# Two raw weight buffers and five split slots in place of three and four

## The chip, the cores and the metric
The kernel runs on 1 core of one Trainium2 chip, as one program. The metric is the device time of one execution in microseconds; the number given for the kernel before is the median of 3 runs.

## The reference, cut to what matters
Two blocks of a language model act one after the other on one sequence of 256 positions, with a model width of 1024, everything in fp32. What matters here is how many different weight matrices it multiplies with: each is used once, by 256 rows.
```python
def first_block(x, mem, ...):               # x, mem: (1, 256, 1024)
    mem_n = rms_norm(mem, mem_norm_gain)
    for layer in range(2):
        g = norm_gains[layer]
        hn = rms_norm(x, g[0])
        y = mlstm_mixer(hn, ...) if layer == 0 else stick_breaking_mixer(hn, ...)
        x = x + rms_norm(y, g[1])
        y = memory_cross_attention(rms_norm(x, g[2]), mem_n, xa_w_q[layer], xa_w_kv[layer], xa_w_o[layer])
        x = x + rms_norm(y, g[3])
        y = swiglu_ffn(rms_norm(x, g[4]), ffn_w_gate_up[layer], ffn_w_down[layer])   # D_FF 2816
        x = x + rms_norm(y, g[5])
    return x

def second_block(x, mem, ...):
    z = _rmsnorm(x, norm_mix_g) @ w_in
    hq, hf, hi, hg, fq, fk, fv, ff, mq, gate_logits = split(z)
    y_a = _hgrn2_mixer(hq, hf, hi, hg, ...)     # chunkwise gated linear attention
    y_b = _fox_mixer(fq, fk, fv, ff, ...)       # softmax attention with forget gates
    y_c = _memory_mixer(mq, _rmsnorm(mem, ...) @ mem_kv_w, ...)
    merged = sum over the three of sigmoid(gate) * (y @ w_br)
    x = x + merged @ w_out
    return x + _conv_glu_ffn(_rmsnorm(x, norm_ffn_g), ffn_w_up, ..., ffn_w_down)
```

## The kernel before, in words
**Weights as a stream.** All weights come from device memory in fp32, in the fixed order in which they are used. `chunk()` (L174 to L202) is called once for each of 207 chunks. A chunk is 1024 KB, that is [128, 2048] on chip, but for two narrow ones of 8 columns each: `mlg` (gate columns of the mLSTM) and `ff` (forget gates of the fox attention). A wide chunk is cut into two pieces of [128, 1024], a narrow one is one piece; there are 412 pieces. Chunk n lies in raw buffer n % NRAW (`raw` is [128, NRAW, 2048] fp32, L100), piece p in slot p % NSP of `whi` and of `wlo` (each [128, NSP, 1024], L101 and L102). A raw buffer and a slot of the two split tiles take the same 8 KB of a partition.

**The split.** TensorE multiplies in a rounded fp32 form, so each weight w is written as a hi part (w rounded) and a lo part (w minus hi), and each product is three matmuls: hi by hi, hi by lo and lo by hi. ACT makes the hi of each piece (a copy, L1149 in `hi_to`), DVE the lo (a subtraction of hi from raw, L1691 in `lo_to`); PE then uses the piece, in order.

**Who waits for what.** SP's program (L2469 to L2489) issues the loads in order. Before the load of chunk c it waits until DVE has made the last lo of chunk c-NRAW (L2474), then issues it (L2480). The two loads of the memory tokens stand in the same queue, right behind `mlg` (L2483). ACT waits at the first piece of a chunk for the landed data (L1146), and for piece p until PE has used piece p-NSP (L1148). DVE waits for the hi. PE waits for the lo. `w_used` counts the pieces that PE is done with.

**Places written out by hand.** ACT and DVE also do everything else: they clear the banks, and compute norms, activations and softmaxes. Each engine takes its instructions strictly in the order in which the program has them, and where the copies and the subtractions stand in it is written out by hand: `past(name)` stands for "make the pieces up to the last one of chunk `name`, plus NSP more" (L1152 for ACT, L1694 for DVE). A call puts all pieces that are not yet made there, each with its waits. So ACT, at a copy whose data has not landed, stands still with everything behind it.

**The order of the work.** mLSTM: `mlq0`, `mlq1`, `mlg`, `mlk0`, `mlk1`, `mlv0a` to `mlo1b` (queries, gates, keys, values, output gates), the decays with exponentials at L1310 to L1314 on ACT and the column tile `acol` on DVE, and PE's log-decay products at L668. Then cross attention (`xq0_0` and on), a feed-forward (`g0_j`, `u0_j`, `d0_j`: gate, up and down chunk of step j), stick-breaking attention (`sbq`, `sbk`, `sbv`, its softmax on ACT, the output weights `sbo0` and on, transposed values in `sb_values`, PE L789), cross attention again (`xq1_0` and on; squares and `norm_hi` at L1181 on ACT before it), a second feed-forward, the second block's mixers (`hq` to `mq`, the six gate blocks `gate0a` to `gate5b`, the branches, `mo`), and the last feed-forward (`g2_j`, `u2_j`, `d2_j`). At the fox attention ACT copies the turned keys (L1515), and `fox_pair` on PE begins with L988. At the last feed-forward's entry the norm of the second 128 rows is copied on ACT in `tile_hi` (L1661), eight copies, and PE's `first_hi` (L437) does the hi products of the first half before they are there. In a feed-forward, DVE clears the gate banks (L1794) and the up banks (L1807), and ACT copies the product for the down matmuls (L1271).

**The narrow pieces.** A narrow piece writes only 16 of the 128 columns of each k-block of its hi slot, but PE's `gate_rows` (L477 to L485) multiplies with all 128 (`both`), so that the other columns only have to be finite numbers. `mlg` is piece 4: slot 0 before the change, which piece 0 has filled.

**Lines of PE.** L407 to L409 are the matmuls of the query and key blocks, L422 and L424 those of the gate and up chunks, L472 to L474 those of the blocks with rows on the partitions.
Of the kernel before, what the change touches and what calls it, by code (L numbers as in the profile page):

```python
# [8 lines left out]
F32 = mybir.dt.float32  # L9
# [8 lines left out]
FF = 2816  # L18
FT = FF // 128
NJ = FT // 2  # L20
NRAW = 3
NSP = 4
NAMES = """
K_act K_dve V_act V_dve act_step constants dve_step f_act f_cols f_conv f_first f_gate f_hi f_lo f_prod
f_tap2 f_up fb_in fx_e fx_m fx_p fx_pa fx_pd fx_s fx_t fx_v g1_in g2_in g3_in gains gains_T gate gb_in h_A
h_A01m h_cp h_d h_e h_f h_m1 h_m2 h_n h_o h_q h_r h_sq h_z half_sq heads_T heads_a heads_d heads_n hg_act
hn_r hn_sq hn_ss ho_r ho_sq ho_ss lg_zero lo_first m2_act m2_dve mT_T mT_hi mT_lo m_T m_hi m_lo m_r m_sq m_x
mem0_in0 mem0_in1 mem1_in0 mem1_in1 mg mg0 ml_act ml_cols ml_dec ml_dve ml_hs ml_log ml_num ml_og ml_p ml_qk
# [63 lines left out]
def build_program(nc, I, out):  # L92
    ctx = ExitStack()
    with ctx:
        def sb(name, shape, dt=F32):
            return ctx.enter_context(nc.sbuf_tensor(name, shape, dt))


        ps = ctx.enter_context(nc.psum_tensor("ps", [128, 8, 512], F32))
        raw = sb("raw", [128, NRAW, 2048])  # L100
        whi = sb("whi", [128, NSP, 1024], F32R)  # L101
        wlo = sb("wlo", [128, NSP, 1024], F32R)  # L102
        xr = sb("xr", [128, NT, D])
# [70 lines left out]
        def chunk(name, src, cut):  # L174
            n = len(order)
            cols, kt = src.shape[1], src.shape[0] // 128
            view = raw[:, n % NRAW, 0:kt * cols].rearrange("p (k c) -> p k c", c=cols)
            if kt * cols <= 1024:
# [6 lines left out]
            if cols == 8:  # L185
                p = len(pieces)
                both = whi[:, p % NSP, :].rearrange("p (k c) -> p k c", c=128)
                if cut == "g":
# [7 lines left out]
            for v in views:  # L196
                p, k, c = len(pieces), v.shape[1], v.shape[2]
                mine.append(Piece(p, n, v, whi[:, p % NSP, 0:k * c].rearrange("p (k c) -> p k c", c=c),
                                  wlo[:, p % NSP, 0:k * c].rearrange("p (k c) -> p k c", c=c)))
                pieces.append(mine[-1])  # L200
# [89 lines left out]
        S = {}  # L290
# [844 lines left out]
        def scalar_program(act):  # L1135
# [3 lines left out]
            def hi_to(n):  # L1139

                while made[0] < min(n, len(pieces)):
                    p = pieces[made[0]]
                    if p.n == 0:
                        act.wait_ge(S["w_first"], 16)
                    elif p.n == 1 or pieces[p.n - 1].of != p.of:
                        act.wait_ge(S[f"w_raw{p.of % NRAW}"], 16 * (p.of // NRAW + 1))  # L1146
                    if p.n >= NSP:
                        act.wait_ge(S["w_used"], p.n - NSP + 1)  # L1148
                    act.activation(p.hi, p.raw, ACT.Copy).then_inc(S["w_hi"], 1)  # L1149
                    made[0] += 1  # L1150

            def past(name):  # L1152

                hi_to(end(name) + NSP)
# [127 lines left out]
            step(act.activation(junk, mhalf[:, :], ACT.Square))  # L1282
            squares(0)
            hi_to(2)
            act.wait_ge(S["gains"], 1)
            norm_hi(0, gain1(0, 0))
            hi_to(4)


# [1027 lines left out]
        def gpsimd_program(pool):  # L2317
            own = [0]

            def step(i):  # L2320
                own[0] += 1
                i.then_inc(S["pool_step"], 1)
                return own[0]
# [27 lines left out]
                    rstd(hn_st[n][t], nh, 512 // nh, "hn_ss", 2 * n + t + 1, "hn_r")  # L2351


            pool.memset(ident[:, :], 0.0)
            z = step(pool.memset(identb[:, :], 0.0))
            pool.memset(mhalf[:, :], -0.5).then_inc(S["mhalf"], 1)
# [112 lines left out]
        def sync_program(sp):  # L2469
            for t in range(NT):  # L2470
                sp.dma_start(xr[:, t, :], x2[:, t, :]).then_inc(S[f"x_in{t}"], 16)
            for c in order:
                if c.n >= NRAW:
                    sp.wait_ge(S["w_lo"], order[c.n - NRAW].end)  # L2474
                src, sem = c.src.rearrange("(k p) c -> p k c", p=128), S[f"w_raw{c.n % NRAW}"]
                if c.n == 0:
# [28 lines left out]
        @block.gpsimd  # L2505
        def _(e):
            gpsimd_program(e)
# [29 lines left out]
```

## Time and profile before
| | |
|---|---|
| median of 3 runs | 1301.5 us (1301.43 to 1301.62) |
| the profiled execution | 1301.93 us, span in the trace 1299.9 us |
| busy share of the span | PE 99%, weight loads of PE 85%, DVE 68%, ACT 53%, POOL 9% |
| granted TensorE clock | the top digit in all 40 slices, mean 1.0 |
| DMA | 223.62 MB, mean 172 GB/s; the queue of the weight loads keeps 16 DMA engines busy for 51.0% |
| weight loads | 1024 KB each, median 5.1 us from issue to landing (6.5 for those of the mLSTM's `w_in`) |

How to read it: the time of an execution is about 2 us more than the span of its trace. PE has work in all but some 18 us of the span. The slices of the page show where PE has less: the first one of 40, with 7 tenths, and no other. The weight load of a matmul (PEld) runs beside the matmul before it, so its idle time costs nothing as long as PE is busy.

### The profile page before, as it was taken

The numbers are of one execution on the slowest core, as the hardware profiler recorded it, in microseconds if no ns is written. First come the engines' busy times: TensorE is split into PE (matmuls) and PEld (weight loads), VectorE is DVE, ScalarE is ACT, GpSimd is POOL, SyncE is SP. The second block draws the span as 40 slices with busy tenths as digits, with TensorE's granted clock in tenths as the row PEclk, the third lists the DMA queues.
The fourth block names the chain that finished last, engine by engine and source line by source line (L and its number), as shares of the span: only waits on it lengthen the run. The fifth ranks groups of instructions, "written<-read, shape, count | busy, mean of one in ns | idle before, by whom it ended". The sixth has DMA issues, their size and how long they took to land.

```text
span 1299.9 us, 17608 instructions
## 1 busy us (share of the span) xinstructions
PE 1281.9 (99%) x7273; PEld 1106.5 (85%) x7273; DVE 883.7 (68%) x1038; ACT 688.1 (53%) x961; POOL 110.7 (9%) x176
## 2 busy tenths in 40 slices
PE   7999999999999999999999999999999999999999
PEld 7888897988888888888888888898877888888887
DVE  4656664776666776875676666768785566887775
ACT  5755544544444656564554444565566654654453
POOL 6200100100000100030100000101330003000000
PEclk9999999999999999999999999999999999999999
DMA  8754643565555553353365555563544435365552
GB/s 265 258 162 157 204 146 126 178 194 195 193 186 185 181 163 129 131 192 132 130 195 193 189 186 183 182 193 106 162 147 147 160 130 194 131 204 186 193 195 97
DMA packets 156112, 223.62 MB, mean 172 GB/s; under 512 B 6103, under 2 KB 107635, under 8 KB 156032
## 3 DMA queue, kind: packets, MB, share of 16 engines
q1 hardware_dynamic: 154240, 218.18, 51.0%
q0 software_dynamic: 1664, 4.27, 1.0%
q8 instruction: 57, 0.93, 0.3%
q14 instruction: 23, 0.19, 0.1%
q10 hardware_dynamic: 128, 0.05, 0.0%
HBM read 221.44 MB, written 1.05 MB: 171 GB/s over the span
## 4 chain that ended last, share of the span: by engine, by line
PE 85%; DVE 7%; ACT 4%; issue 2%; POOL 1%; DMA 1%; SPq 0%; POOLq 0%; ACTq 0%; DVEq 0%
PE ps L422 18%; PE ps L424 9%; PE ps L472 8%; PE ps L474 7%; PE ps L473 7%; PE ps L407 5%; PE ps L409 5%; PE ps L408 5%; PE ps L606 4%; PE ps L607 4%; PE ps L608 4%; DVE wlo L1691 3%; ACT whi L1149 2%; PE ps L493 1%; PE ps L541 1%
## 5 line engine op out<-in xcount | busy, mean ns | idle before, releaser
L1691 DVE TENSOR_TENSOR wlo<-raw,whi 128x1024 fp32r<-128x1024 f32 x409 | 491.6, 1231 | 167.9 <-ACT whi L1149 165.1
L1149 ACT ACTIVATE whi<-raw 128x1024 fp32r<-128x1024 f32 x412 | 425.5, 1052 | 334.7 <-PE ps L422 156.1
L422 PE MATMUL ps<-RR,whi 128*128 128x512 f32 x1024 | 353.8, 396 | 0.7 <-DVE ar L1794 0.7
L424 PE MATMUL ps<-RR,wlo 128*128 128x256 f32 x1024 | 264.8, 279 | 0.1
L472 PE MATMUL ps<-whi,RR 128*128 128x512 f32 x592 | 238.2, 402 | 2.1 <-DVE RR L1968 0.4
L474 PE MATMUL ps<-whi,RR 128*128 128x512 f32 x592 | 231.0, 390 | 0.0
L473 PE MATMUL ps<-wlo,RR 128*128 128x512 f32 x592 | 230.9, 390 | 0.0
L422 PEld LDWEIGHTS ps<-RR,whi 128*128 128x128 f32 x1024 | 184.8, 188 | 36.3 <-DVE ar L1794 1.0
L424 PEld LDWEIGHTS ps<-RR,wlo 128*128 128x128 f32 x1024 | 193.0, 188 | 11.9 <-DVE RR L1721 0.4
L407 PE MATMUL ps<-RR,whi 128*128 128x256 f32 x512 | 147.4, 288 | 1.5 <-DVE RR L1721 1.4
L409 PE MATMUL ps<-RR,wlo 128*128 128x256 f32 x512 | 144.8, 283 | 0.0
L408 PE MATMUL ps<-RR,whi 128*128 128x256 f32 x512 | 144.8, 283 | 0.0
L472 PEld LDWEIGHTS ps<-whi,RR 128*128 128x128 f32 x592 | 111.2, 188 | 29.3 <-issue 4.1
L474 PEld LDWEIGHTS ps<-whi,RR 128*128 128x128 f32 x592 | 111.1, 188 | 24.1
L473 PEld LDWEIGHTS ps<-wlo,RR 128*128 128x128 f32 x592 | 111.3, 188 | 21.3
L407 PEld LDWEIGHTS ps<-RR,whi 128*128 128x128 f32 x512 | 98.1, 192 | 4.5 <-DVE RR L1721 2.9
L606 PE MATMUL ps<-whi,RR 128*128 128x512 f32 x256 | 99.7, 389 | 0.0
L608 PE MATMUL ps<-whi,RR 128*128 128x512 f32 x256 | 99.6, 389 | 0.0
L607 PE MATMUL ps<-wlo,RR 128*128 128x512 f32 x256 | 99.6, 389 | 0.0
L408 PEld LDWEIGHTS ps<-RR,whi 128*128 128x128 f32 x512 | 98.1, 192 | 0.2
L409 PEld LDWEIGHTS ps<-RR,wlo 128*128 128x128 f32 x512 | 98.1, 192 | 0.0
L1794 DVE TENSOR_REDUCE ar<-ps 128x512 f32<-128x1024 f32 x33 | 40.4, 1224 | 72.1 <-PE ps L422 71.7
(338 smaller groups left out, 1266.7 us busy)
## 6 DMA issues: line engine op xcount, KB each, us to landing
raw<-in_ffn_w_gate_up SPq DMA_DIRECT2D x44, 1024.0 KB, 5.1
raw<-in_ffn_w_down SPq DMA_DIRECT2D x33, 1024.0 KB, 5.0
raw<-in_w_in SPq DMA_DIRECT2D x28, 1024.0 KB, 5.1
raw<-in_ffn_w_up SPq DMA_DIRECT2D x22, 1024.0 KB, 5.1
raw<-in_xa_w_kv SPq DMA_DIRECT2D x16, 1024.0 KB, 5.2
raw<-in_sb_w_qkv SPq DMA_DIRECT2D x12, 1024.0 KB, 5.1
raw<-in_ml_w_in SPq DMA_DIRECT2D x11, 1024.0 KB, 6.5
raw<-in_xa_w_q SPq DMA_DIRECT2D x8, 1024.0 KB, 5.3
```

Of the source, the lines that this page charges most:

```text
L407: pe.matmul(o, p.hi[:, k, :], X.h[:, k, :], start=k == 0, stop=False)
L408: pe.matmul(o, p.hi[:, k, :], X.l[:, k, :], start=False, stop=False)
L409: m = pe.matmul(o, p.lo[:, k, :], X.h[:, k, :], start=False, stop=k == 7)
L422: m = pe.matmul(two(ps[:, bank, :]), p.hi[:, k, :], XT2[:, k, :, :], start=k == 0, stop=k == 7)
L424: pe.matmul(ps[:, bank, 0:256], p.lo[:, k, :], X.h[:, k, :], start=False, stop=False)
L472: pe.matmul(o, X.h[:, g, r], p.hi[:, k, :], start=g == 0, stop=False)
L473: pe.matmul(o, X.h[:, g, r], p.lo[:, k, :], start=False, stop=False)
L474: m = pe.matmul(o, X.l[:, g, r], p.hi[:, k, :], start=False, stop=g == K - 1)
L606: pe.matmul(o, h[:, i, r], p.hi[:, 0, c], start=j == 0 and i == 0, stop=False)
L607: pe.matmul(o, h[:, i, r], p.lo[:, 0, c], start=False, stop=False)
L1149: act.activation(p.hi, p.raw, ACT.Copy).then_inc(S["w_hi"], 1)
L1691: dve.tensor_tensor(p.lo, p.raw, p.hi.bitcast(F32), ALU.subtract).then_inc(S["w_lo"], 2 if p.n == 2 else 1)
```

## The change
NRAW goes from 3 to 2 and NSP from 4 to 5. The memory of the third raw buffer holds the fifth slot of `whi` and `wlo`. As every place of a copy or subtraction (`past`), every slot wait and every load's wait is written with these two constants, they all shift with them. Piece 4, the narrow one, now is the first to use slot 4, which nothing has written before; so POOL fills that slot with zeros ahead of its other work, and ACT waits for it before the hi of piece 4.
```diff
@@ -18,11 +18,11 @@
-NRAW = 3
-NSP = 4
+NRAW = 2
+NSP = 5
 NAMES = """
...
@@ -1144,6 +1144,8 @@
                         act.wait_ge(S["w_first"], 16)
                     elif p.n == 1 or pieces[p.n - 1].of != p.of:
                         act.wait_ge(S[f"w_raw{p.of % NRAW}"], 16 * (p.of // NRAW + 1))
+                    if p.n == 4:
+                        act.wait_ge(S["g_zero"], 1)
                     if p.n >= NSP:
                         act.wait_ge(S["w_used"], p.n - NSP + 1)
                     act.activation(p.hi, p.raw, ACT.Copy).then_inc(S["w_hi"], 1)
@@ -2351,6 +2353,7 @@
                     rstd(hn_st[n][t], nh, 512 // nh, "hn_ss", 2 * n + t + 1, "hn_r")
 
 
+            pool.memset(whi[:, 4, :].bitcast(F32), 0.0).then_inc(S["g_zero"], 1)
             pool.memset(ident[:, :], 0.0)
             z = step(pool.memset(identb[:, :], 0.0))
             pool.memset(mhalf[:, :], -0.5).then_inc(S["mhalf"], 1)
```

## Rows read from the trace of the kernel before
**Rows 1.** Part 1 of the page: busy us (share of the span) and instructions.
```profile
PE 1281.9 (99%) x7273; PEld 1106.5 (85%) x7273; DVE 883.7 (68%) x1038; ACT 688.1 (53%) x961; POOL 110.7 (9%) x176
```

**Rows 2.** Part 5 of the page: group, busy, mean ns, idle before, releaser.
```profile
L1149 ACT ACTIVATE whi<-raw 128x1024 fp32r<-128x1024 f32 x412 | 425.5, 1052 | 334.7 <-PE ps L422 156.1
```

**Rows 3.** Waits: engine line <- waited for: us in total, times, longest.
```profile
ACT whi L1149 <- DMA raw<-in_ml_w_in: 9.6, 5, 6.0
...
SPq L2480 <- DVE wlo L1691: 1177.3, 201, 17.4
...
PEld ps L472 <- DVE wlo L1691: 2.2, 3, 0.8
```

**Rows 4.** The loads issued by L2480, all of them.
```profile
DMA to landing us min/median/max: 2.2/5.1/10.8
```

**Rows 5.** Timeline, ACT and DVE, 299 to 318: start, us, instructions, [idle <-releaser].
```profile
299.84 1.99 ACT L1149 ACTIVATE whi<-raw 128x1024 fp32r<-128x1024 f32 x2
...
312.94 2.35 DVE L1691 TENSOR_TENSOR wlo<-raw,whi 128x1024 fp32r<-128x1024 f32 x2
...
315.93 0.63 ACT L1271 ACTIVATE RR<-ar 128x512 fp32r<-128x512 f32 x1 [3.07 <-DVE ar L1811]
...
316.46 1.99 ACT L1149 ACTIVATE whi<-raw 128x1024 fp32r<-128x1024 f32 x2
```

**Rows 6.** Timeline, ACT and DVE at the last feed-forward's entry.
```profile
1111.85 2.00 ACT L1149 ACTIVATE whi<-raw 128x1024 fp32r<-128x1024 f32 x2
...
1113.20 1.22 DVE L1691 TENSOR_TENSOR wlo<-raw,whi 128x1024 fp32r<-128x1024 f32 x1
...
1127.72 1.22 DVE L1807 TENSOR_REDUCE ar<-ps 128x512 f32<-128x1024 f32 x1
```

**Rows 7.** The chain that ended last, the same place: start, us, what.
```profile
1114.44 5.75 PE ps L437 x48
```

**Rows 8.** Timeline at the fox attention's entry.
```profile
946.09 2.22 ACT L1149 ACTIVATE whi<-raw 128x1024 fp32r<-128x1024 f32 x2
...
947.96 2.35 DVE L1691 TENSOR_TENSOR wlo<-raw,whi 128x1024 fp32r<-128x1024 f32 x2
...
961.85 0.22 PE L988 MATMUL ps<-mRow,identb 128*128 128x128 bf16 x1 [0.46 <-DVE Kx L2103]
```

**Rows 9.** Timeline of the start.
```profile
16.41 0.96 POOL L2378 MEMSET Kx<- 128x1024 f32 x1
...
22.65 2.01 ACT L1149 ACTIVATE whi<-raw 128x1024 fp32r<-128x1024 f32 x2 [5.97 <-DMA raw<-in_ml_w_in]
...
26.23 0.28 PE L407 MATMUL ps<-RR,whi 128*128 128x256 f32 x1
...
26.70 1.06 ACT L1149 ACTIVATE whi<-raw 128x1024 fp32r<-128x1024 f32 x1 [2.04 <-DMA raw<-in_ml_w_in]
...
49.93 1.28 ACT L1310 ACT_TABLE_LOAD   x1
...
52.97 0.23 PE L668 MATMUL ps<-mInc,identb 128*128 128x128 bf16 x1
```

**Rows 10.** Timeline at the end of the stick-breaking attention.
```profile
524.17 4.62 DVE L1691 TENSOR_TENSOR wlo<-raw,whi 128x1024 fp32r<-128x1024 f32 x4
...
524.44 1.99 ACT L1149 ACTIVATE whi<-raw 128x1024 fp32r<-128x1024 f32 x2
...
529.23 0.66 PE L789 MATMUL ps<-ar 128*64 128x256 f32 x4
```

**Rows 11.** Timeline at the norm before the second cross attention.
```profile
566.13 2.35 DVE L1691 TENSOR_TENSOR wlo<-raw,whi 128x1024 fp32r<-128x1024 f32 x2
...
567.31 1.99 ACT L1149 ACTIVATE whi<-raw 128x1024 fp32r<-128x1024 f32 x2
...
571.70 0.84 ACT L1181 ACTIVATE RR<-ps,gcol 128x256 fp32r<-128x256 f32 x2 [0.32 <-PE ps L493]
...
574.81 0.28 PE L407 MATMUL ps<-RR,whi 128*128 128x256 f32 x1
```

More of the change, by code:

```diff
@@ L20 @@
 NJ = FT // 2
-NRAW = 3
-NSP = 4
+NRAW = 2
+NSP = 5
 NAMES = """
 K_act K_dve V_act V_dve act_step constants dve_step f_act f_cols f_conv f_first f_gate f_hi f_lo f_prod
-f_tap2 f_up fb_in fx_e fx_m fx_p fx_pa fx_pd fx_s fx_t fx_v g1_in g2_in g3_in gains gains_T gate gb_in h_A
+f_tap2 f_up fb_in fx_e fx_m fx_p fx_pa fx_pd fx_s fx_t fx_v g1_in g2_in g3_in g_zero gains gains_T gate gb_in h_A
 h_A01m h_cp h_d h_e h_f h_m1 h_m2 h_n h_o h_q h_r h_sq h_z half_sq heads_T heads_a heads_d heads_n hg_act
```

## The prediction
> **What bounds the kernel now.** I read the page first. PE is busy for 1281.9 of 1299.9 us [rows 1], so nearly any idle time the change puts on PE is added to the total, and there are only 18 us of it to win, of which the start and the store at the end have most. Next the group of the hi copies on ACT: 412 of them, 1052 ns each, with 334.7 us of idle time before them, mostly for PE [rows 2]: a copy waits until a slot is free, not for weights. Then the waits: ACT waited for raw data for 9.6 us in all, with ml_w_in at the start and never again; SP, which issues the weight loads, stands 1177.3 us in 201 waits for DVE's lo subtraction; and PE's weight loads waited for a lo piece for 2.2 us in all [rows 3]. So raw data is early and split pieces are nearly always there in time. From issue to landing a chunk takes 5.1 us in the median [rows 4]; that is the price on which everything below rests. Last I read the timelines of ACT and DVE around each stage change, to see what stands right behind a copy in ACT's queue.
>
> **What the change moves.** past(name) makes pieces up to end(name)+NSP, and piece p waits for w_used at p-NSP+1. With five slots piece p therefore takes the place in ACT's and DVE's queues, and the slot wait, that piece p-1 has now. PE gets one piece more of lead; no wait of another instruction becomes shorter, since each past() still waits for the same use. For the raw buffers the trade is worse than one for one. Chunk c now goes where c-3 was; after the change it waits for the second lo of c-2, which is made where the first lo of c-2 is made now. And its first copy stands where ACT now starts the second copy of c-1. So, for every chunk: new landing = end of the first lo of c-2 today + 5.1; wanted = start of the second copy of c-1 today. The difference is how long ACT, whose queue is in order, stands still with all that is behind.
>
> **The feed-forward stages** (some 550 us): take a down chunk around 315 us. The lo that frees its buffer ends at 314.1 (first of the pair at 312.94), it lands at 319.2 and is wanted at 317.4, the second copy of the pair at 316.46 [rows 5]: 1.8 us late. ACT has idle time in every such step, 3.07 us before L1271 alone [rows 5], and PE uses the piece at least three pieces (8 us) later. A step of three chunks takes 16.6 us (the pairs at 299.84 and 316.46 [rows 5]), two chunks 11. Two buffers turn in 5.1 us plus a copy and two subtractions in chain, some 3.5 us: 8.6 us. I cost these stages at nothing: the cover is the slot lead. If it were gone, the 1.8 us of each chunk would be paid (rival 3).
>
> **The last feed-forward's entry.** Chunk g2_1 takes g2_0's buffer: the latter's first lo runs 1113.20 to 1114.42 and holds the place of the second after the change, so g2_1 lands at 1119.5. ACT wants it at 1112.8 (second of the two copies at 1111.85), and right behind stand the eight copies of the second half's norm, which start when the pair is done, at 1113.9 [rows 6]. They start at 1120.6. PE has two pieces of the first half to do (a third of the 5.75 us of L437 [rows 7], 1.9 us) and then waits from 1116.1 to 1121.4: 5.3 us. The next chunk is freed only behind that norm and delays L1807, which clears the banks for u2_1 and starts at 1127.72 today [rows 6]: 1.4 us more. Sum 6.7.
>
> **The fox attention's entry.** gate0a is freed by the lo that ends at 949.17 (first of the pair at 947.96), lands at 954.3, and is wanted at 947.25, the second copy at 946.09 [rows 8]. Behind it stand the value eviction, the four y copies and, through DVE, two more lo. Then gate0b, freed at about 961, lands at 966, again ahead of the two key copies (L1515) that fox_pair waits for. PE, which starts L988 at 961.85 after 0.46 us of idle [rows 8], starts it at about 969.2: 7.3 us, with nothing ahead of it in its own order to fill them.
>
> **The start.** mlg and the two mem loads now go out only when the lo of piece 2 is made, at 17 us, ahead of mlk0. So mem takes the place of mlk0 in the transfers (landed before the copy at 22.65) and mlk0 that of mlk1 (26.70) [rows 9]. Its first lo comes at 28.7 instead of 25.0, and PE wants it at 26.23: 2.4 us. Then the ring of two is short of data: in the same way mlk1 lands at 29, mlv0a at 35, mlv0b at 38, mlv1a at 46, mlv1b at 53, mlo0a at 59. The first piece of mlo0a stands ahead of the decay exponentials (the table load at 49.93 today) and, on DVE, ahead of acol; PE's L668 after 52.97 [rows 9] waits for that. It would come some 8.8 us late in all; bounds 2.4 (the later lateness is hidden) and 13 (the four gain row loads slow the chunks: the slowest landing today took 10.8 us [rows 4]). I take 9. The new memset is POOL's first work. One of the same size took 0.96 us [rows 9], and the first of its results is wanted after 2 us by ACT, whose table load covers it: nothing, at most 0.96.
>
> **Stick-breaking attention.** sbo1 is freed at 525.4 (first lo of the four at 524.17), lands at 530.5, wanted at 525.4 (second copy at 524.44), 5.1 late. Behind it are the eviction that sb_values(4) needs (PE at 529.23) and three activations of a softmax that have under 1 us of slack at the last pair [rows 10]: 3.0 + 0.8. The same place at 479 us is 4.4 late and costs 1.4. Together 5.2.
>
> **The norms.** At xq1_1: freed at 567.35, landed 572.45, wanted 568.3; behind it 2.1 us of squares and the norm's copies (571.70, then 575.7). PE starts xq1_0 at 574.81 and needs three of eight lo [rows 11]: 2.8. The same pattern stands at five other norms: 1.4 each at 440, 651 and 847 us (late 2.6, 4.0, 4.0, less the idle ACT has there), 0.5 at 163, 0 at 240. Two more, at the head gain (116 us) and the first query eviction (587 us), take 1.1 and 1.0; one before the second fox weights (1023 us), 1.3. Together 2.8 + 4.2 + 0.5 + 3.4 = 10.9.
>
> **Sum.** 6.7 + 7.3 + 9 + 5.2 + 10.9 = 39.1 us. Gain on the other side: at most the 2.2 us of [rows 3], taken as 0, since a weight load runs beside the matmuls. The profiled execution took 1301.93 us (span 1299.9), 0.4 above the median of 1301.5: I put the sum on the median, **1340.6 us**. Ends: each term down to nothing but the two large ones and the start at 2.4 gives +16.4; all terms, 4 us more at the start and a little more at each of the dozen places where a landing takes 6 us instead of 5.1 give +56.
>
> **A rule against the trace.** The landing of 5.1 us is a median over all stages [rows 4]. The Trainium skill (DMA: Bandwidth & Descriptors, Anatomy of one DMA) fits a DMA as 2.0 us plus bytes over 436 GB/s, measured on the other issue path; an estimate by it is 4.4 us for this chunk, and each of a dozen places would be 0.7 us cheaper, some 31 us in all. The measured landing decides.
>
> **Rivals.**
> 1. Two buffers are enough: where a landing is late ACT finds idle time or PE has other work, as in the feed-forwards. For it speaks that raw data never made ACT wait after the start [rows 3]. Against it, the four stretches above, in which a bound PE waits within 1 us of the late instruction today. Then only the 2.4 us at the start remain or not even they: 1301.5 to 1304. The Trainium skill (Trainium Kernel Development and Optimization, Best Practices) says to double-buffer so that DMA overlaps compute, which by itself would call the third buffer spare and the time 1301.5. Chance 0.05.
> 2. Faster: the fifth slot feeds PE wherever it waits for pieces. Its price is the 2.2 us of [rows 3] and perhaps as much in the gaps after them: 1298.5. It decides if the landings stay ahead of ACT, which the rows above speak against. Chance 0.04.
> 3. Ring starved: the lateness adds up in the feed-forwards because copy, subtraction and landing form one chain. 99 chunks at 1.8 us give +178: about 1480. Half of it: 1410. Against it the 8.6 against 11 us. Chance 0.08.
>
> The forecast has 0.83, of which some 0.07 lie beyond its own ends. **Range** 1315 to 1362. A measurement of this kernel tells 0.2% (2.6 us) from no change. Faster 0.04, within 0.2% 0.04, slower 0.92.
>
> **What would show it.** ACT's idle time before L1149 for the raw load: 9.6 us now [rows 3], well over 100 us then. SP's longest waits shorter, each issue right after a second lo. PE idle of about 7 us before L988, 5 before L437, 3 before the transposed values after 529 us, over 5 before L668. The feed-forward steps still 16.6 us for three chunks; if they are longer, rival 3. If PE's idle stays at 18 us, the order argument is wrong and rival 1 or 2 holds. If the sites are there but shorter, the landing is cheaper than 5.1.

## The result and the profile after

The changed kernel takes 1353.3 us (median of 5 runs, 1350.7 to 1358.0) against 1301.5 us; the ratio is 1.0407, 95% interval 1.0385 to 1.0428. Its profiled execution took 1353.05 us, its span is 1350.4 us. The range of 1315 to 1362 holds it; the forecast of 1340.6 is 12.7 us short.

The first part of the page, against [rows 1], says where that is:
```profile
span 1350.4 us, 17610 instructions
...
PE 1293.8 (96%) x7273; PEld 1114.4 (83%) x7273; DVE 888.1 (66%) x1038; ACT 679.7 (50%) x961; POOL 106.8 (8%) x177
```
The span grew by 50.5 us. PE's time without work grew from 18.0 us (1299.9 less 1281.9) to 56.6 us, by 38.6. The remaining 11.9 us are PE's busy time: the same 7273 matmuls took longer. The forecast had a sum of 39.1 us for the first and nothing for the second.

The group of the hi copies, against [rows 2], now waits for loads instead of for PE (part 5 of the page; then the view of waits: us in total, times, longest):
```profile
L1151 ACT ACTIVATE whi<-raw 128x1024 fp32r<-128x1024 f32 x412 | 426.0, 1051 | 456.9 <-DMA raw<-in_ffn_w_gate_up 127.2
```
```profile
ACT whi L1151 <- DMA raw<-in_ffn_w_gate_up: 127.2, 41, 5.4
...
ACT whi L1151 <- DMA raw<-in_ffn_w_down: 49.8, 30, 4.5
ACT whi L1151 <- DMA raw<-in_ffn_w_up: 49.0, 20, 6.8
...
ACT whi L1151 <- DMA raw<-in_ml_w_in: 26.9, 8, 7.4
...
ACT whi L1151 <- DMA raw<-in_xa_w_q: 20.1, 5, 5.7
```
Waits for raw data were 9.6 us in [rows 3] and are 273 in the rows shown alone. Most of that, the 226 us of the three feed-forward lines, cost nothing, but for those at the stages' entries (6.8 us at the last one, below). From the last use of u0_2's first piece to that of d0_10's first piece passed 150.75 us before and after, 149.35 us in the second feed-forward and 127.27 us in the third, to a hundredth. The loads themselves are as quick as in [rows 4], issued by L2483 now:
```profile
DMA to landing us min/median/max: 2.2/5.1/9.9
```
So the loss is at the stage changes. The timeline at the last feed-forward's entry, against [rows 6] and [rows 7]:
```profile
1155.08 1.05 ACT L1151 ACTIVATE whi<-raw 128x1024 fp32r<-128x1024 f32 x1
...
1162.92 1.06 ACT L1151 ACTIVATE whi<-raw 128x1024 fp32r<-128x1024 f32 x1 [6.79 <-DMA raw<-in_ffn_w_up]
1163.88 0.61 ACT L1663 ACTIVATE RR<-ps,gcol 128x128 fp32r<-128x128 f32 x2
...
1156.44 1.22 DVE L1693 TENSOR_TENSOR wlo<-raw,whi 128x1024 fp32r<-128x1024 f32 x1
...
1157.42 2.15 PE L437 MATMUL ps<-RR,whi 128*128 128x256 f32 x16
1164.67 6.01 PE L437 MATMUL ps<-RR,whi 128*128 128x256 f32 x32 [5.10 <-DVE RR L2297]
```
The subtraction that frees g2_1's buffer ends at 1157.66, the load lands 5.2 us later, ACT stands still for 6.79 us with the norm copies (L1663) behind it, and PE waits 5.10 us before L437. The 32 matmuls behind the wait take 6.01 us where 16 before it took 2.15: 188 ns each instead of 134. The windows view of PE shows why (stretch, length, PE busy with its matmuls, granted clock, DMA share, GB/s):
```profile
1158.00:1160.00 2.00, 1.57 (x14) 1.00 0.49 141
1160.00:1162.00 2.00, 0.00 (x0) 1.00 1.07 372
1162.00:1164.00 2.00, 0.00 (x0) 0.56 0.04 11
1164.00:1166.00 2.00, 1.33 (x6) 0.50 0.00 0
1166.00:1168.00 2.00, 2.00 (x11) 0.50 0.00 0
1168.00:1170.00 2.00, 2.00 (x15) 0.73 0.00 0
1170.00:1172.00 2.00, 2.00 (x19) 1.00 0.70 208
```
The granted clock went to the lower level, 1.2 GHz, while PE stood idle, and was back at 2.4 GHz only after 1168, some 4 us into the work. In the kernel before every stretch of 2 us up to 1298 shows 1.00; only the last, behind the end of PE's work at 1296.8, shows 0.69. The Trainium skill (TensorE: Matmul & The Clock Gate, Part 1) says that the clock is a gate with these two levels which activity opens and idleness closes; the windows agree.

The start and the fox entry, against [rows 9] and [rows 8] (timelines of ACT and PE):
```profile
26.73 2.00 ACT L1151 ACTIVATE whi<-raw 128x1024 fp32r<-128x1024 f32 x2 [7.43 <-DMA raw<-in_ml_w_in]
...
62.11 1.06 ACT L1151 ACTIVATE whi<-raw 128x1024 fp32r<-128x1024 f32 x1 [5.92 <-DMA raw<-in_ml_w_in]
...
986.98 1.06 ACT L1151 ACTIVATE whi<-raw 128x1024 fp32r<-128x1024 f32 x1 [7.18 <-DMA raw<-in_w_in]
...
29.10 0.58 PE L407 MATMUL ps<-RR,whi 128*128 128x256 f32 x1 [2.87 <-DVE wlo L1693]
...
64.57 0.29 PE L668 MATMUL ps<-mInc,identb 128*128 128x128 bf16 x1 [6.21 <-DVE st L1856]
...
991.84 1.97 PE L493 MATMUL ps<-ident,ar 128*128 128x128 f32 x8 [4.33 <-DVE RR L1723]
1001.52 0.22 PE L988 MATMUL ps<-mRow,identb 128*128 128x128 bf16 x1 [1.64 <-DVE Kx L2105]
```
Set against the steps of the prediction, the sites come out so. "Growth" is how much later PE finished with the piece there than before, less the same for the piece ahead of it; "slower work" is the growth less the idle time added.

| site | forecast | idle time added | slower work | growth |
|---|---|---|---|---|
| start: mlk0 | 2.4 | 2.9 | 1.7 | 4.6 |
| start: before L668 (and 0.5 before L472) | 6.6 | 6.7 | 3.0 | 9.7 |
| stick-breaking: before L789, twice | 5.2 | 4.5 | 0.1 | 4.6 |
| norm ahead of xq1_0 | 2.8 | 3.5 | 1.8 | 5.3 |
| fox: before L493 and L988 | 7.3 | 5.5 | 1.7 | 7.2 |
| last feed-forward's entry | 6.7 | 5.1 | 2.2 | 7.3 |
| the other norms, gains, gates | 8.1 | 10.4 (the rest) | 1.4 (the rest) | 11.8 (the rest) |
| all | 39.1 | 38.6 | 11.9 | 50.5 |

In the five rows with 1.7 to 3.0 us the granted clock is at its lower level behind the wait. The 0.1 and the 1.4 us are not the clock, which stays at 1.00 there (it is lower once more behind the end of PE's work): the first matmuls behind each wait take some 0.1 to 0.3 us longer than before.

### The profile page after: what moved, and what is told of

It is laid out like the page before. It is cut to its first block, busy times and chain, and to the rows that moved or that the text cites. A ratio compares the mean times of both kernels' runs of the same rounds, so it can differ in the third digit from the quotient of the medians.

```text
span 1350.4 us, 17610 instructions
## 1 busy us (share of the span) xinstructions
PE 1293.8 (96%) x7273; PEld 1114.4 (83%) x7273; DVE 888.1 (66%) x1038; ACT 679.7 (50%) x961; POOL 106.8 (8%) x177
## 4 chain that ended last, share of the span: by engine, by line
PE 66%; DVE 12%; DMA 10%; ACT 8%; issue 3%; POOL 1%; SPq 0%; POOLq 0%; ACTq 0%; DVEq 0%
PE ps L422 17%; PE ps L424 9%; DVE wlo L1693 5%; PE ps L472 5%; PE ps L473 5%; PE ps L474 5%; PE ps L606 4%; PE ps L608 4%; PE ps L607 4%; ACT whi L1151 4%; PE ps L407 3%; PE ps L409 3%; PE ps L408 3%; DMA raw<-in_ml_w_in 3%; DMA raw<-in_w_in 2%
## 5 line engine op out<-in xcount | busy, mean ns | idle before, releaser
L1693 DVE TENSOR_TENSOR wlo<-raw,whi 128x1024 fp32r<-128x1024 f32 x409 | 499.5, 1235 | 286.6 <-ACT whi L1151 286.0
L422 PE MATMUL ps<-RR,whi 128*128 128x512 f32 x1024 | 354.0, 396 | 1.5 <-DVE RR L1723 0.7
L472 PE MATMUL ps<-whi,RR 128*128 128x512 f32 x592 | 239.4, 404 | 2.5 <-DVE ar L1756 0.5
L422 PEld LDWEIGHTS ps<-RR,whi 128*128 128x128 f32 x1024 | 184.8, 188 | 37.6 <-issue 1.1
L407 PE MATMUL ps<-RR,whi 128*128 128x256 f32 x512 | 149.2, 291 | 11.1 <-DVE RR L1723 8.2
L408 PE MATMUL ps<-RR,whi 128*128 128x256 f32 x512 | 146.1, 285 | 0.0
L472 PEld LDWEIGHTS ps<-whi,RR 128*128 128x128 f32 x592 | 112.1, 189 | 29.5 <-issue 3.8
L2331 POOL TENSOR_SCALAR st<-st 128x1 f32<-128x1 f32 (+2 forms) x42 | 17.3, 412 | 837.4 <-ACT xn L1199 698.8
```

The lines of the kernel that those rows point to most:

```text
L407: pe.matmul(o, p.hi[:, k, :], X.h[:, k, :], start=k == 0, stop=False)
L408: pe.matmul(o, p.hi[:, k, :], X.l[:, k, :], start=False, stop=False)
L422: m = pe.matmul(two(ps[:, bank, :]), p.hi[:, k, :], XT2[:, k, :, :], start=k == 0, stop=k == 7)
L472: pe.matmul(o, X.h[:, g, r], p.hi[:, k, :], start=g == 0, stop=False)
L1693: dve.tensor_tensor(p.lo, p.raw, p.hi.bitcast(F32), ALU.subtract).then_inc(S["w_lo"], 2 if p.n == 2 else 1)
```

## The experiments

Each is the median of 4 to 11 runs, to be set against a median of the kernel before of 1301.5 us. It was 1301.65 beside four of them: the half loads in the kernel before, the later memory tokens with half loads and with the places of four, and the fill alone.

**Two raw buffers, four slots.**
```diff
-NRAW = 3
+NRAW = 2
 NSP = 4
```


> The kernel before with two raw buffers and still four slots; no other edit. Theory P (the places do it): a chunk is now issued after the second lo of the chunk two before it, as late as after the change, but its first copy keeps its place of today, one copy later than after the change. From the times of the kernel before with 5.1 us of landing, the chunks that land too late are 11 instead of 118, and their lateness adds up to 33 us instead of 261; at the five sites that cost most after the change the lateness is 0.5 (start), none (exponentials), none (second cross attention's norm), none and 0.9 (fox), 2.1 (last feed-forward, for a copy behind the norm). So 1302 to 1309, about 1305. Rival R (a third raw buffer is needed wherever the copies stand): most of the loss is here too, 1330 to 1350.

Measured 1310.9 us (1307.6 to 1311.9), ratio 1.0064 (1.0052 to 1.0077): a fifth of the loss, though 2 us above the range I gave. Waits for raw data in its view of waits are small and many:
```profile
ACT whi L1149 <- DMA raw<-in_ffn_w_down: 38.0, 22, 1.9
ACT whi L1149 <- DMA raw<-in_ml_w_in: 19.7, 7, 7.2
ACT whi L1149 <- DMA raw<-in_ffn_w_gate_up: 16.9, 10, 5.5
```
PE has three waits that the kernel before doesn't: 2.92 us before mlk0, with 1.5 us of clock behind it, 1.15 before L472 at the `ff` piece, and 2.87 (0.75 before) before L422 at the first gate chunk behind the last norm, where g2_1 is late behind the norm. The last was in the list of late chunks (2.1 us) but I had taken it as covered. The loss of the third buffer by itself is therefore worth 9.4 us by the medians (6.1 to 10.4 over the runs), not 50. What else the change does must carry the rest.

**Two raw buffers, five slots, the places as before.**
```diff
+LEAD = 4
...
-                hi_to(end(name) + NSP)
+                hi_to(end(name) + LEAD)
...
-                lo_to(end(name) + NSP)
+                lo_to(end(name) + LEAD)
```
(and so in the ten other calls that name NSP by hand; the slot wait and the slots keep NSP = 5)

> The changed kernel (two raw buffers, five slots), but the hand-written places of the copies and subtractions count four pieces ahead as in the kernel before; only the slot waits see the fifth slot. Theory P: the loss goes as with two buffers and four slots, 1302 to 1308, and not below the kernel before, since PE has only some 4 us of idle time there that better supply could remove. Rival R: 1330 to 1350. Rival S (the fifth slot itself, its zeroing or its addresses cost something): stays above the run with four slots by more than 3 us.

Measured 1305.9 us (1304.5 to 1306.4), ratio 1.0029 (1.0018 to 1.0040). With all the memory moved as in the change, only the places of the copies put back, 47.4 of the 51.8 us are gone. Memory, zeroing and addresses are not the cause (rival S falls). With two buffers, the places are; early places with three buffers were not run.

**One copy put back at one site.**
```diff
-            past("mo3")
+            hi_to(end("mo3") + NSP - 1)
             tile_hi(1, gain2(32))
```


> The changed kernel with one copy put back: at the last feed-forward's entry ACT makes one piece less before the second half of the norm (the first piece of g2_1 goes behind the eight norm copies, where it stood before). Theory P: the 5.1 us of idle time before L437 and the 2.2 us that the lowered clock costs behind it are gone, and some 0 to 1 us returns at the next step: 1346 to 1348. Rival (that wait is set by something else, such as the norm's statistics): 1352 to 1356.

Measured 1345.6 us (1344.1 to 1349.2), 7.7 us below the changed kernel and 0.4 below my range. The timeline of ACT and PE there:
```profile
1154.21 1.05 ACT L1151 ACTIVATE whi<-raw 128x1024 fp32r<-128x1024 f32 x1
1156.30 0.62 ACT L1663 ACTIVATE RR<-ps,gcol 128x128 fp32r<-128x128 f32 x2 [1.03 <-PE ps L1115]
...
1161.81 1.06 ACT L1151 ACTIVATE whi<-raw 128x1024 fp32r<-128x1024 f32 x1 [2.67 <-DMA raw<-in_ffn_w_up]
...
1156.56 5.99 PE L437 MATMUL ps<-RR,whi 128*128 128x256 f32 x48
```
All 48 matmuls of L437 run without a wait, in 5.99 us, and the growth at this site is 7.27 us smaller than in the changed kernel, which is the 5.10 of idle time and the 2.2 of clock. One instruction in another order is worth 7.3 us here.

**Each chunk as two half loads.**
```diff
-                views = [view[:, :, 0:cols // 2], view[:, :, cols // 2:cols]]
+                views = [raw[:, n % NRAW, 1024 * i:1024 * i + 1024].rearrange("p (k c) -> p k c", c=cols // 2) for i in range(2)]
...
-                if c.n >= NRAW:
-                    sp.wait_ge(S["w_lo"], order[c.n - NRAW].end)
...
-                sp.dma_start(c.view, src).then_inc(sem, 16)
+                for i, p in enumerate(c.pieces):
+                    if c.n >= NRAW:
+                        old = order[c.n - NRAW]
+                        sp.wait_ge(S["w_lo"], old.pieces[i].n + 1)
+                    sp.dma_start(p.raw, part).then_inc(S[f"w_half{i}{c.n % NRAW}"], 16)
```
(narrow chunks left out here; ACT waits for the half of each piece)

> The changed kernel (two raw buffers, five slots, copies placed five ahead), with every chunk loaded as two transfers of 512 KB, one for each piece; each half is issued as soon as the lo of the piece that lay there is made, so a load no longer waits for the second lo of a chunk. The halves of a raw buffer are laid one behind the other. Theory P says that the loss is the time from that lo to the landing against the place of the copy: a half is issued one subtraction earlier and is half as long. With an estimated 3.8 us of landing (between the 2.2 us of the shortest load and the 5.1 us of a whole chunk) no chunk would be late by the times of the kernel before; at 4.8 us a handful by up to 1 us. So 1302 to 1308; what stays is the start (mlk0 behind the memory tokens, 2 to 4 us). Rival: two buffers are too few bytes in flight, or the short rows of the halves (512 bytes) make the transfers slower: above 1320.

Measured 1304.0 us (1303.4 to 1306.0), ratio 1.0021 (1.0012 to 1.0030). Same buffers, same slots, same early places, and 49.3 of 51.8 us are gone. ACT's waits for raw data and the loads of the page's part 6:
```profile
ACT whi L1159 <- DMA raw<-in_ml_w_in: 16.3, 9, 5.6
ACT whi L1159 <- DMA raw<-in_ffn_w_gate_up: 6.2, 3, 2.4
```
```profile
raw<-in_ffn_w_gate_up SPq DMA_DIRECT2D x88, 512.0 KB, 4.5
raw<-in_ffn_w_down SPq DMA_DIRECT2D x66, 512.0 KB, 4.2
```
Half the bytes land only 0.6 and 0.8 us sooner in these two rows (5.1 and 5.0 for a whole chunk). So I put most of the gain down to each half being issued a subtraction earlier; no run has the one without the other. The Trainium skill (DMA: Bandwidth & Descriptors, Anatomy of one DMA) fits a fixed 2.0 us and a part by bytes, measured on the other issue path, which makes 3.2 us of 512 KB by an estimate; the rows have 4.2 to 4.5, so the fit is too quick for both sizes here, and my 3.8 was too.

**Half loads in the kernel before.**
The same edit on three raw buffers and four slots.

> The kernel before (three raw buffers, four slots) with half loads alone. Raw data is early there already, so a theory in which the half loads only mend what the change broke gives 1300.9 to 1302. If twice as many transfers or their short rows cost something, it shows here without cover: above 1303.

Measured 1302.1 us (1301.4 to 1303.8) against 1301.65, ratio 1.0006 (0.9997 to 1.0015): no difference that can be told, so twice the transfers are free here and bring nothing where loads are early.

**The memory tokens later.**
```diff
-                if c is C["mlg"]:
+                if c is C["mlk1"]:
                     for t in range(NT):
                         sp.dma_start(mem_tm[:, t, :], m1[:, t, :]).then_inc(S[f"mem0_in{t}"], 16)
```


> The changed kernel with the two loads of the memory tokens issued behind mlk1 instead of behind mlg. My step said that they take the place of mlk0 in the transfers. Then the 2.9 us of idle time before mlk0's first matmul and the 1.5 us of the lowered clock behind it are gone: 1348 to 1350 beside the changed kernel's 1353.3 (of which up to 1 us may come back at the exponentials). Rival (mlk0 is late because of the ring of two alone): no change at that place, 1352 to 1355.

Measured 1352.3 us (1351.7 to 1354.8), above the range I gave and inside the rival's, though its condition is not met: at mlk0 the growth fell by 3.8 us and the wait from 2.87 to 0.49 us, so the tokens' loads were its cause. But of these 3.8 us, 1.0 came back before L472 and some more before L668. The net of the start was 2.8 us, and in the profiled execution the clock fell once more elsewhere, behind the wait before L988, which cost 3.8 us.

With half loads and with the places of four:

> The changed kernel with half loads (1304.0) and the memory tokens loaded behind mlk1. In the run with half loads alone the only step that stands out against the kernel before is mlk0: 1.8 us of idle time and 1.7 us of the lowered clock, 3.5 in all. With whole chunks, moving the memory tokens took 3.8 us off that place, and later chunks of the start, short of data, gave most of it back. With halves the later ones have room: 1300.5 to 1301.5, within 0.1% of the kernel before. Rival (the start gives it back here too): 1303 to 1304.5.

> Two raw buffers, five slots, copies placed four ahead (1305.9), and the memory tokens loaded behind mlk1. Its steps against the kernel before were 2.7 at mlk0 and 3.7 at u2_0 (a wait of 2.9 us and the lowered clock), less 3 us gained in small steps by the earlier slots. Without the first: 1302.5 to 1304. Rival (given back within the start): 1305 to 1306.5.

Measured 1303.0 us (1302.4 to 1304.0), ratio 1.0010 (1.0001 to 1.0019), and 1303.0 us (1300.8 to 1305.5), ratio 1.0007 (0.9998 to 1.0016). The first is 1.5 us above what I expected, although mlk0's growth is gone in its trace; the second is as expected. Neither beats the kernel before. What the profile of the second shows, taken in its slowest run (1305.5 us), is one wait of 3.18 us before the gate matmuls behind the last norm, with the lower clock behind it; up to there the earlier slots had brought PE 1.9 us ahead of the kernel before.

**The fill alone.**
```diff
+            pool.memset(whi[:, 3, :].bitcast(F32), 0.0).then_inc(S["g_zero"], 1)
             pool.memset(ident[:, :], 0.0)
...
+                    if p.n == 3:
+                        act.wait_ge(S["g_zero"], 1)
```


> The kernel before with the fill alone: POOL fills one slot with zeros (slot 3, first used by piece 3) ahead of its other work, and ACT waits for it before that piece. My step took this as nothing, at most 0.96 us: 1301.3 to 1302.5. Rival (the fill holds back POOL's first results, which ACT and PE wait for at the start): +1 us or more, above 1302.5.

Measured 1301.64 us against 1301.65, ratio 0.9997 (0.9988 to 1.0006). Nothing, as costed.

**The clock: a wait put into the kernel before.** Two kernels with in-place copies on ACT:
```diff
             past("mo3")
+            for x in (Kx, Vx):      # delay6: (Kx, grow)
+                x = x[:, :, :].rearrange("p a b -> p (a b)")
+                act.activation(x, x, ACT.Copy)
             tile_hi(1, gain2(32))
```


> The kernel before with two in-place copies added on ACT (4.1 us together, values unchanged) right before the second half's norm copies at the last feed-forward's entry. PE has 1.9 us of other work there, so it stands still for about 2.3 us. If the place of the wait is the whole price, +2.3 us: 1303.8. If the clock falls behind a wait as short as this, 1 to 2 us more: 1305 to 1306.

> The same with 6.1 us of copies. PE stands still for about 4.3 us before L437. Theory C (a wait of this length is followed by a stretch at the lower clock, 2 us dear, as in the changed kernel): the step of mo3's last use grows by 6 to 6.6 us and the time is 1307.5 to 1308.5, with a granted clock near 0.5 for some 5 us behind the wait. Rival (the clock fell for another reason in the changed kernel): +4.3 us, 1305.8, clock 1.0 throughout.

Measured 1304.9 us (1303.6 to 1305.3) and 1306.7 us (1306.4 to 1307.6), ratios 1.0023 and 1.0041. The timeline and the windows of PE in the shorter one:
```profile
1113.89 2.15 PE L437 MATMUL ps<-RR,whi 128*128 128x256 f32 x16
1117.84 4.39 PE L437 MATMUL ps<-RR,whi 128*128 128x256 f32 x22 [1.80 <-DVE RR L2298]
```
```profile
1118.00:1120.00 2.00, 2.00 (x12) 0.63 0.00 0
1120.00:1122.00 2.00, 2.00 (x12) 0.51 0.00 0
1122.00:1124.00 2.00, 2.00 (x19) 1.00 0.71 217
```
The waits are 1.80 and 3.50 us; in both the clock is at the lower level behind them, and the growth at the site (3.55 and 5.25 us) is 1.75 us more than the wait. So such a wait costs itself and then some 1.7 us, at this site even where it is 1.80 us long. The waits are shorter than I had said (2.3 and 4.3), since the copies were: the two of the longer kernel took 1.91 and 3.61 us. That is why the shorter kernel came out 0.1 us below its range for a falling clock and the longer one 0.8 us below the range of theory C; its rival had the clock at 1.0 throughout, which it isn't.

**The clock: PE's waits filled.** The changed kernel with matmuls whose results are thrown away, at five waits; one of the five:
```diff
+            def fill(o, X, n):
+                for i in range(n):
+                    pe.matmul(o, X.h[:, 0, 0:128], X.h[:, 1, :], start=True, stop=True)
...
+            fill(ps[:, 3, 0:256], X, 22)
             fm("mlk0", X, 3)
```


> The changed kernel with matmuls added at five of PE's waits (before mlk0, before the fourth log-decay product, before xq1_0, before the fox key transposes, before the last feed-forward's second half norm): about as long as the wait, their results thrown away. PE's idle time rose by 38.6 us after the change, and its busy time by 11.9 us with the same instructions; in the trace the granted clock is at about 0.5 for some 4 to 6 us behind each of these five waits and nowhere else. Theory C (the clock is lowered because PE stood idle): with the waits filled the granted clock stays at 1.0, the same instructions take 9 to 12 us less, 1341 to 1346, and the runs scatter less than the 7 us of the changed kernel. Rival: the clock falls for another reason, 1352 to 1358.

Measured 1354.5 us (1352.8 to 1356.4): no gain, and outside the 1341 to 1346 of theory C. At the five sites it did what theory C says: the windows there are at 1.00 and the growth fell by 1.3 (mlk0), 4.1 (L668), 1.6 (xq1), 1.7 (L493) and 2.2 us (L437), 10.9 in all. But it came back at others, in the timelines of ACT (the load of sbk0 landed late) and PE, and the windows of PE:
```profile
452.47 1.06 ACT L1171 ACTIVATE whi<-raw 128x1024 fp32r<-128x1024 f32 x1 [4.15 <-DMA raw<-in_sb_w_qkv]
...
456.92 0.39 PE L411 MATMUL ps<-RR,whi 128*128 128x256 f32 x1 [3.29 <-DVE RR L1743]
...
1001.00 0.27 PE L1004 MATMUL ps<-mRow,identb 128*128 128x128 bf16 x1 [2.84 <-DVE Kx L2125]
```
```profile
458.00:460.00 2.00, 2.00 (x12) 0.50 0.00 0
...
552.00:554.00 2.00, 2.00 (x12) 0.50 0.00 0
...
1002.00:1004.00 2.00, 2.00 (x12) 0.50 0.47 107
```
At 1001 the reason can be read: fox_pair (L988, here L1004) waits for a chain of ACT and DVE that did not move, so a faster PE came earlier and waited 2.84 us instead of 1.64. It then met the lower clock there (growth 4.2 us more). Two other waits, of 3.29 and 3.00 us, were followed by the lower clock in this execution, where the changed kernel's had 1.60 and 3.08 us and no fall (growth 3.2 and 2.6 us more). With the 1.1 us that came back beside L668, the four make up for the 10.9. So theory C holds at a site and was wrong as a sum: with a dozen waits of 1 to 3 us left, there are other places for the clock to fall, and, as at 1001, a wait for a chain of ACT and DVE takes back what PE was quicker by.

## Why the prediction was right, and what it left out

**The frame held.** The median landing stayed 5.1 us, and the sum of PE's added idle time was forecast at 39.1 us and is 38.6. That the two sums agree to 0.5 us is partly luck: by site the forecast is off by 0.1 to 2.3 us, to both sides, and the misses cancel. That the total still came out 12.7 us short is the missing term below; the width of the range, set for other reasons, covered it.

**The feed-forwards at nothing: right.** The three stretches kept their times to a hundredth, over 427 us, though ACT waited for loads in most steps. Rival 3 is out. ACT's idle time was the cover, with the slots' lead behind it.

**The stage changes: right in place, near in size.** The last entry was forecast with 5.3 us before L437 and 1.4 us at L1807: the first is 5.10, the second did not show (0.73 before L422, where the kernel before has 0.75). At the start, 2.4 and 6.6 against 2.9 and 6.7. At the fox entry the 7.3 us did not stand before L988 as I wrote: 4.33 of them come before the key transposes (L493) one step ahead, which wait for the y copies that I had named as standing behind gate0a, and 1.2 before L988. Stick-breaking 4.5 for 5.2. The small sites were too cheap by 2.3 us in sum: the head gain cost 2.0 for 1.1, the place before the second fox weights 2.1 for 1.3, and a wait of 1.26 us before L951 was not on my list.

**The term that was missing: the clock.** The step "PE's idle time is added to the total" is true but not the whole: the work behind a wait also ran slower. Five waits of 2.9 to 6.2 us in the changed kernel are followed by windows at 1.2 GHz and cost 10.4 of the 11.9 us of added busy time. The page of the kernel before showed the clock at its top digit in every slice, and I did not ask what it would do at waits that the kernel didn't have yet. Its trace had a hint, at its only long waits, in the first 8 us, and at the same work later:
```profile
8.08 3.67 PE L493 MATMUL ps<-ident,xn 128*128 128x128 f32 x16 [2.74 <-DVE xn L1711]
...
570.30 1.91 PE L493 MATMUL ps<-ident,xn 128*128 128x128 f32 x16
```
The same 16 matmuls take 1.76 us more at the start. The view of windows gives 1.00 there, so that this is the clock is not shown; but 1.8 us for each of five larger waits would have put 9 us into the sum, of the 10.4 measured.

**Rival 1** (two buffers are enough) was closer than its chance says, in another sense than I gave it: two buffers are nearly enough (1305.9 us) if the copies stand where they stood, and with half loads (1304.0) even if they don't. **Rival 2**, that the fifth slot feeds PE, has a trace of truth: in the kernel with the old places small gains of 0.3 to 0.8 us bring PE from 2.9 us behind the kernel before (after mlk0) to 0.8 us ahead of it, 3.7 us in all and more than the 2.2 I had given as the most; the wait before L422 and the clock behind it then take 3.7 back. In **rival 3** "half of it: 1410" is a slip: half of 178 us makes 1390.

**What stays open.** Which wait is followed by the lower clock in a given execution: those of 3.08 us (changed kernel), 2.87 (two buffers, four slots) and 2.42 (places of four, before mlk0) were not, those of 1.80 were. It goes with the scatter of 7 us among the changed kernel's runs: their mean granted clock is 0.992, 0.991 and 0.990 at spans of 1348.9, 1350.4 and 1351.6 us, and 0.986 and 0.987 at 1355.6 and 1356.2. A mean lower by 0.006 of 1350 us is 8 us of work, about the 7 seen. In the kernel with two buffers and four slots it is likewise 1.000 at 1305.7 us and 0.996 at 1310.2. Where the clock fell in those runs is not known, since one execution of each kernel was profiled. The kernel before has no such fall and yet scatters by 2.1 us (1301.1 to 1303.2 over 33 runs). Three raw buffers with five slots were not tried, as the fifth slot takes the third buffer's memory, nor was the opposite trade, four raw buffers and three slots.

## What to carry to other kernels

Where buffer counts also set the places of instructions in an in-order queue, a change of counts is a change of order: write for each load the end of the instruction that frees its buffer, add the landing, and compare with the new place of its first use; then look at what stands right behind that use. Splitting a load so that each part is issued when its own part of the buffer is free was worth nearly as much here as a third buffer (1304.0 against 1301.5 us). And when a change will make a busy PE wait, add to each of the longer waits the price of the work behind it at the lower clock, which was 1.7 to 3.0 us a wait here.

## What the runs showed of the hardware that I had not expected

A wait of 1.80 us before L437 was followed by matmuls mostly at half clock (22 in 4.39 us, 200 ns each, against 134 ns ahead of it), 1.75 us dear; the clock was granted at 1.00 during the wait itself and fell in the stretch behind it. Three waits of 2.42 to 3.08 us in other kernels were followed by none. And a 512 KB load took 4.2 to 4.5 us to land where one of 1024 KB took 5.0 to 5.1.
